# One group of products instead of two for the four finest levels of a gated recurrence, and their four masked copies behind it

## The chip, the cores and the metric

The kernel runs on one core of one Trainium2 chip. What is measured is the time of one execution on the device, in microseconds (us); the time before is the median of three runs. The engines are called PE (TensorE), DVE (VectorE), ACT (ScalarE), POOL (GpSimd) and SP (SyncE).

## The reference

The model is a chain of layers over 256 positions of width 2048: a convolution mixer, a gated recurrence (HGRN2), a sliding-window attention and a gated feed-forward. The change is in the recurrence. It has 16 heads of 128 channels and runs over the positions forward and backward:

```
b = cumsum(log_f)                                  # per channel
decay[t, s] = exp(b[t] - b[s]) where s <= t        # per channel
scores[t, s] = sum_k q[t, k] * key[s, k] * decay[t, s, k]
out[t] = sum_s scores[t, s] * v[s]                 # and the state of the chunks before
```

What is computed is one 256 x 256 matrix of weights per head (lower triangle from the forward pass, upper one from the backward pass, the sum of both on the diagonal), times v. Around it stand a projection in front (q, two gates, v and an output gate z from the normed input), a norm per head, the product with silu(z), and a projection behind.

## The kernel before, in words

Every weight matrix comes in chunks of 256 rows by 512 columns (SP's DMA into `raw`). ACT rounds a chunk to `w_hi` (L928), DVE subtracts to get the rest `w_lo` (L1319), and PE multiplies: three products for each of four pieces, `w_hi` with the high part of the activations (L662), `w_lo` with it (L663), and `w_hi` with their low part (L664). That is 12 products of 512 columns a chunk. There are four slots. PE waits for `split_ready`, ACT for `chunk_used` of four chunks before.

Each phase of the kernel is a `stream` of chunks, 32 in one pass of the recurrence's projection, and each engine runs the same stream. Other work hangs on it by hand: `Hooks().put(tick, step)` makes an engine do a step right behind its own work on chunk number `tick`. The order on each engine is therefore fixed, and engines meet by semaphores only. ACT and DVE can be up to some three chunks ahead of PE.

The recurrence works on four heads at a time, a head group j. While the projection of head group j + 1 (for the last one: of z) streams through PE, `process(j)` is hooked in. The weight matrix of a head is built by halving: level 1 is the block between the two halves of 128 positions, level 2 that between quarters (64), and so on down to neighbours (level 8, `LEVELS` = 64 to 1 for s = 2 to 8); level 0 is the diagonal. The steps of a level s >= 2 are:

- DVE `diffs` (L1567 to L1570) writes differences of the summed gates for queries and keys into one of four operand buffers, `operands(s)` in `E` and `E_more`; ACT `exp` (L1138) exponentiates them; DVE `weigh` (L1578) multiplies the queries by q.
- PE `level(j, s)` (L777) makes 32 small products (four heads, two halves, four quarters of 32 rows; for s = 2 16 of 64) into bank `2 + s % 2` of the PSUM tile `T`, columns 0 to 255. It waits for `weigh` (`g_G`), for the keys' exponentials (`g_K`), and for the copies out of the bank up to level s - 2 (`g_S`).
- A copy takes the level out of PSUM: for levels 0 to 3 on ACT (L1144 to L1155), for levels 4 to 8 DVE `take` (L1586, L1587). The latter is a drain, a memset of two elements and a copy under a mask into the blocks `SB`; a level's mask picks its elements.

When all five are in, ACT `blocks` (L1163, four copies) puts `SB` into the weight matrices `ST`. PE multiplies these by v: `av_across` (L787), which needs only level 1, and `av` (L789), which needs the blocks.

PE's ticks are: level 0 at 8, level 1 at 13, level 2 at 14, levels 3 and 4 at 18, 5 and 6 at 22, 7 and 8 at 26, then `av_across` at 26 and `av` at 28. DVE's `weigh` of level s is at 11 + 2s, its `diffs` of level s + 1 at 12 + 2s, its copies are at 21 (level 4), 25 (5 and 6, before the `weigh` of 7) and 29 (7 and 8). ACT's `exp` of level s is at 11 + 2s, `blocks` at 29. DVE's quarters of the next head group (L1628) are at 28, 30 and 31. For the last head group DVE's first gate of the output (L1644) is at 29, behind the copies.

Of the kernel before, what the change touches and what calls it, by code (L numbers as in the profile page):

```python
# [36 lines left out]
S = 256  # L37
# [22 lines left out]
QUARTER = P // 4  # L60
# [4 lines left out]
ACT_TAKES = 4  # L65
# [111 lines left out]
def build(nc, t, out):  # L177
    ph = phases()
    ctx = ExitStack()
    with ctx:  # L180
# [3 lines left out]
        def sem(name):  # L184
            return ctx.enter_context(nc.semaphore(name))
# [102 lines left out]
        T = ctx.enter_context(nc.psum_tensor("T", [P, 4, 512], F32))  # L288
# [3 lines left out]
        def operands(s):  # L292

            b = (s - 1) % 4 if s else 1
            return (E_more if b >= 2 else E)[:, b % 2, :, :, :]

        def gate_banks(k):
            return T01 if k % 2 else T23
# [19 lines left out]
        g_raw, g_q, g_M, g_act, g_lb, g_D, g_E, g_G, g_mm, g_S = (  # L318
            sem(f"hgrn_{s}") for s in ("raw", "quarters", "moved", "act", "lb", "D", "E", "G", "mm", "S"))
# [287 lines left out]
        def _(pe):  # L607
# [86 lines left out]
            def v_turn(j):  # L694
                if is_first(j):
                    pe.wait_ge(small_in, 16)
                pe.wait_ge(c_v, j + 1)
                if not is_first(j):
                    pe.wait_ge(c_pad, 2 * j)
                transposes(T01, atok, c_T)  # L700
# [43 lines left out]
            at = Hooks().put(4, lambda: v_turn(3))  # L744
# [11 lines left out]
            def level(j, s):  # L756

                pe.wait_ge(g_G, 9 * j + s + 1)
                if s == 0:
                    pe.wait_ge(g_M, 3 * j + 3)  # L760
                if s >= 2:
                    pe.wait_ge(g_K, 7 * j + s - 1)
                    pe.wait_ge(g_S, 9 * j + s - 1)
                e = operands(s)
                for h in range(HPG):
                    for b in range(2):
                        if s == 1:
                            last = nc.tensor.matmul(T[:, h // 2, (h % 2) * S + b * P:(h % 2) * S + b * P + P],  # L768
                                                    e[:, 0, h, b * P:(b + 1) * P], e[:, 1, h, (1 - b) * P:(2 - b) * P],
                                                    start=True, stop=True)  # L770
                            continue
                        n = HB if s == 2 else QUARTER
                        for i in range(P // n):
                            at = b * P + i * n
                            to = b * P + (i ^ 1) * n if s in (2, 3) else at
                            g, q = (e[:, 1, h, at:at + n], qT[:, h, to:to + n]) if s == 0 else (e[:, 0, h, at:at + n], e[:, 1, h, to:to + n])
                            last = nc.tensor.matmul(T[i * n:(i + 1) * n, 2 + s % 2, (2 * h + b) * n:(2 * h + b + 1) * n],  # L777
                                                    g, q, start=True, stop=True)
                last.then_inc(g_mm, 1)

# [11 lines left out]
            def av_across(j):  # L792
                pe.wait_ge(g_raw, 4 * j + 4)
                pe.wait_ge(g_S, 9 * j + 2)
                av_products(True)

            def av(j):
                pe.wait_ge(g_sb, j + 1)
                av_products(False).then_inc(g_av, 1)

            def process(j):

                at = Hooks().put(8, lambda: level(j, 0))
                for s in range(1, 9):
                    at.put(13 if s == 1 else 10 + 4 * (s // 2 + s % 2) if s > 2 else 14, lambda s=s: level(j, s))
                return at.put(26, lambda: av_across(j)).put(28, lambda: av(j))

            def qaai(j):
# [14 lines left out]
            at = process(3)  # L823
# [61 lines left out]
            at = Hooks().put(14, k_turn)  # L885
# [412 lines left out]
        def _(dve):  # L1298
# [4 lines left out]
            def settle():  # L1303

                return nc.vector.drain()  # L1305
# [114 lines left out]
            at = Hooks()  # L1420
# [59 lines left out]
            at = Hooks()  # L1480
# [14 lines left out]
            def bounds_of(j):  # L1495

                if not is_first(j):
                    dve.wait_ge(g_act, 6 * j)
                V.tensor_copy(lbj[:, :, :, :], lbt[:, :, :, bass.ds(4 * j, 4)]).then_inc(g_lb, 1)

            def diagonal_f(j):

                dve.wait_ge(g_lb, j + 1)
                dve.wait_ge(g_act, 6 * j + 1)
                for h in range(HPG):
                    V.tensor_scalar(E[:, 1, 1, h, :], kf[:, h, :], lbj[:, 0, 1, h:h + 1], None, ALU.mult)
                settle()

            def diagonal_b(j):

                dve.wait_ge(g_act, 6 * j + 3)
                for h in range(HPG):
                    last = STT(out=E[:, 1, 1, h, :], in0=kb[:, h, :], scalar=lbj[:, 1, 1, h:h + 1],
                               in1=E[:, 1, 1, h, :], op0=ALU.mult, op1=ALU.add)
                last.then_inc(g_G, 1)

            def scan_f(j):

                dve.wait_ge(g_act, 6 * j + 2)
                for h in range(HPG):  # L1520
                    V.tensor_tensor_scan(Bc[:, h, :], Bc[:, h, :], Bc[:, h, :], 0.0, ALU.add, ALU.bypass)

            def scan_b(j):

                dve.wait_ge(g_act, 6 * j + 4)
                lf = lf_back
                for h in range(HPG):
                    V.tensor_tensor_scan(Xc[:, h, 1:S], lf[:, h, 0:S - 1], lf[:, h, 0:S - 1], 0.0, ALU.add, ALU.bypass)
                V.memset(Xc[:, :, 0:1], 0.0)
                settle()  # L1530

            def keys(j, d):

                dve.wait_ge(g_act, 6 * j + 5 + d)
                if d == 0:
                    TT(kf[:, :, :], kf[:, :, :], Bc[:, :, :], ALU.subtract)
                else:
                    TT(kb[:, :, :], kb[:, :, :], Xc[:, :, :], ALU.add)
                    V.tensor_scalar(back[:, 0, :], Bc[:, :, P - 1], -1.0, None, ALU.mult)
                    V.tensor_scalar(back[:, 1, :], Xc[:, :, P], -1.0, None, ALU.mult)  # L1540
                    settle().then_inc(g_D, 1)
# [30 lines left out]
            def weigh(j, s):  # L1572

                e = operands(s)
                dve.wait_ge(g_E, 8 * j + s)
                if s == 1:
                    dve.wait_ge(g_M, 3 * j + 3)
                TT(e[:, 1, :, :], e[:, 1, :, :], qT[:, :, :], ALU.mult).then_inc(g_G, 1)  # L1578

            def take(j, s):  # L1580

                settle()
                if s == ACT_TAKES:
                    dve.wait_ge(g_S, 9 * j + s)
                dve.wait_ge(g_mm, 9 * j + s + 1)
                V.memset(none[:, :], 0.0)  # L1586
                V.copy_predicated(SB[:, :, :, :].rearrange("p a b c -> p (a b) c"),  # L1587
                                  lmask[:, s - ACT_TAKES, :].unsqueeze(1).to_broadcast([P, 8, QUARTER]),
                                  T[:, 2 + s % 2, 0:S].rearrange("p (a c) -> p a c", c=QUARTER)).then_inc(g_S, 1)

            def o_norm(j):
                dve.wait_ge(g_o, 2 * (j + 1))
# [12 lines left out]
            def process(j, scale_later=0):  # L1605
                at = Hooks().put(1, lambda: bounds_of(j)).put(3, lambda: diagonal_f(j)).put(5, lambda: scan_f(j)).put(6, lambda: diagonal_b(j)).put(9, lambda: scan_b(j))
                at.put(10, lambda: keys(j, 0)).put(11, lambda: keys(j, 1)).put(12, lambda: diffs(j, 2))
                for s in range(1, 9):
                    if s > ACT_TAKES and s % 2:
                        for done in range(max(ACT_TAKES, s - 2), s):  # L1610
                            at.put(11 + 2 * s, lambda done=done: take(j, done))
                    at.put(11 + 2 * s, lambda s=s: weigh(j, s))
                    if 2 <= s < 8:
                        at.put(12 + 2 * s, lambda s=s: diffs(j, s + 1))
                at.put(29, lambda: take(j, 7)).put(29, lambda: take(j, 8))
                return at.put(32, lambda: o_norm(j)).put(33 + scale_later, lambda: o_scale(j))

            def rest(j):
                return Hooks() if isinstance(j, int) and j < 0 else process(j).later(32)
# [31 lines left out]
            at = Hooks().put(32, lambda: z_lo(0)).with_(process(3, 1)).with_(rest(2))  # L1651
# [135 lines left out]
            at = Hooks()  # L1787
# [49 lines left out]
            at = Hooks().put(2, lambda: u_out(FJ - 1)).put(3, lambda: f_quarters(FJ - 1)).put(13, lambda: f_lo_out(FJ - 1))  # L1837
# [52 lines left out]
```

## Time and profile before

| | us |
|---|---|
| median of three runs | 1887.22 (1886.92 to 1888.4) |
| the profiled execution | 1887.1 |
| its span, first to last instruction | 1885.3 |
| PE busy | 1880.2 |
| DVE busy | 1313.4 |
| ACT busy | 1065.9 |
| POOL busy | 689.0 |

The clock granted to PE was full over the whole span. The four head groups stand in the trace at about 477 to 544, 576 to 644, 675 to 743 and 775 to 843 us. A product of fp32 operands, as L777, L787 and L789 make them, stands in the trace as two records, each with its own load of weights, so a level of 32 products is 64 records. Times in the rows are the starts from the span's beginning; ends of products are modelled, and a product of 512 columns is shown as 0.39 us long though the next one starts sooner. "issue" means that nothing shown was waited for.

### The profile page before, as it was taken

Reading aid. Unit: us, or ns where it says so; the run is one execution under the profiler, and the core shown is the slowest. Engines: PE = TensorE matmul, PEld = TensorE weight load, DVE = VectorE, ACT = ScalarE, POOL = GpSimd, SP = SyncE. Lnnn points to the kernel's source line nnn. Section 1 sums busy time; section 2 is a strip of 40 time slices with the busy share of each in tenths; the row PEclk is TensorE's granted clock in tenths of the full one; section 3 lists DMA queues with packets and bytes.
Section 4 is the critical chain, followed back from the end, with each engine's and each line's share of the span. In section 5 each row is a group of like instructions: output and inputs, shape, how many; then the busy total and the mean of one; then the engine's idle time right before and its main releaser. Section 6 shows DMA issues by size and latency. Waiting matters only on the chain.

```text
span 1885.3 us, 29572 instructions
## 1 busy us (share of the span) xinstructions
PE 1880.2 (100%) x11192; PEld 1552.3 (82%) x11192; DVE 1313.4 (70%) x1887; ACT 1065.9 (57%) x1408; POOL 689.0 (37%) x749
## 2 busy tenths in 40 slices
PE   9999999999999999999999999999999999999999
PEld 8888878888888888888887888888888888888887
DVE  5899988746888888887668887655555555544443
ACT  7444466546878787975455756444444444443332
POOL 1899884606051423302418647322222222210000
PEclk9999999999999999999999999999999999999999
DMA  9666656666555565555565455666666666665664
GB/s 328 193 190 190 179 175 201 194 191 179 173 172 170 159 180 167 178 160 177 190 196 151 153 185 176 207 198 189 190 196 193 191 196 192 192 195 192 194 195 159
DMA packets 183603, 352.69 MB, mean 187 GB/s; under 512 B 11840, under 2 KB 12352, under 8 KB 183488
## 3 DMA queue, kind: packets, MB, share of 16 engines
q1 hardware_dynamic: 183344, 351.12, 61.1%
q8 instruction: 75, 1.23, 0.3%
q14 instruction: 40, 0.33, 0.1%
q10 hardware_dynamic: 144, 0.01, 0.0%
HBM read 348.99 MB, written 2.10 MB: 186 GB/s over the span
## 4 chain that ended last, share of the span: by engine, by line
PE 99%; DVE 1%; issue 0%; ACT 0%; POOL 0%; DVEq 0%; POOLq 0%
PE acc L662 32%; PE acc L664 31%; PE acc L663 31%; PE T L777 1%; PE T L613 1%; PE acc L629 1%; PE T L859 0%; PE T L882 0%; PE T L787 0%; PE T L789 0%; PE T L768 0%; PE T L620 0%; DVE cy L1444 0%; DVE w_lo L1319 0%; PE T L736 0%; PE T L725 0%
## 5 line engine op out<-in xcount | busy, mean ns | idle before, releaser
L1319 DVE TENSOR_TENSOR w_lo<-raw,w_hi 128x1024 fp32r<-128x1024 f32 x564 | 702.3, 1248 | 495.7 <-ACT w_hi L928 485.8
L928 ACT ACTIVATE w_hi<-raw 128x1024 fp32r<-128x1024 f32 x655 | 686.9, 1057 | 589.2 <-PE acc L664 565.1
L662 PE MATMUL acc<-w_hi,h_hi 128*128 128x512 f32 x1872 | 734.2, 392 | 0.0
L664 PE MATMUL acc<-w_hi,h_lo 128*128 128x512 f32 x1872 | 728.7, 389 | 0.0
L663 PE MATMUL acc<-w_lo,h_hi 128*128 128x512 f32 x1872 | 728.6, 389 | 0.0
L662 PEld LDWEIGHTS acc<-w_hi,h_hi 128*128 128x128 f32 x1872 | 351.4, 188 | 76.4 <-issue 3.3
L664 PEld LDWEIGHTS acc<-w_hi,h_lo 128*128 128x128 f32 x1872 | 351.3, 188 | 73.6
L663 PEld LDWEIGHTS acc<-w_lo,h_hi 128*128 128x128 f32 x1872 | 351.5, 188 | 71.4
L602 POOL COPY fT<-fq 32x256 f32<-32x256 f32 x176 | 111.7, 635 | 360.0 <-DVE fq L1822 353.1
L502 POOL TENSOR_TENSOR w_lo<-raw,w_hi 128x1024 fp32r<-128x1024 f32 x76 | 181.0, 2412 | 62.5 <-ACT w_hi L928 62.3
L1410 DVE SCALAR_TENSOR_TENSOR T<-vpad,feat,T 128x256 f32<-128x256 f32 x464 | 182.4, 480 | 0.0
L662 PE MATMUL acc<-w_hi,y_hi 128*128 128x512 f32 x384 | 150.5, 392 | 0.4 <-DVE y_lo L1324 0.4
L663 PE MATMUL acc<-w_lo,y_hi 128*128 128x512 f32 x384 | 149.5, 389 | 0.0
L662 PE MATMUL acc<-w_hi,f_hi 128*128 128x512 f32 x352 | 136.9, 389 | 0.0
L663 PE MATMUL acc<-w_lo,f_hi 128*128 128x512 f32 x352 | 136.9, 389 | 0.0
L664 PE MATMUL acc<-w_hi,f_lo 128*128 128x512 f32 x352 | 136.9, 389 | 0.0
L540 POOL COPY kf<-sz 32x256 f32<-32x256 f32 x64 | 37.3, 583 | 249.2 <-DVEq L1305 246.7
L664 PE MATMUL acc<-w_hi,hy_lo 128*128 128x512 f32 x256 | 99.7, 389 | 0.0
L662 PEld LDWEIGHTS acc<-w_hi,y_hi 128*128 128x128 f32 x384 | 72.1, 188 | 16.8 <-DVE y_lo L1324 1.1
L663 PEld LDWEIGHTS acc<-w_lo,y_hi 128*128 128x128 f32 x384 | 72.1, 188 | 14.7
L663 PEld LDWEIGHTS acc<-w_lo,f_hi 128*128 128x128 f32 x352 | 66.1, 188 | 13.8
L664 PEld LDWEIGHTS acc<-w_hi,f_lo 128*128 128x128 f32 x352 | 66.1, 188 | 13.7
(268 smaller groups left out, 1642.7 us busy)
## 6 DMA issues: line engine op xcount, KB each, us to landing
raw<-in_hgrn_w_in_dram SPq DMA_DIRECT2D x160, 512.0 KB, 3.7
raw<-in_conv_w_in_dram SPq DMA_DIRECT2D x96, 512.0 KB, 4.3
raw<-in_ffn_w_gate_dram SPq DMA_DIRECT2D x88, 512.0 KB, 4.4
raw<-in_ffn_w_up_dram SPq DMA_DIRECT2D x88, 512.0 KB, 4.2
raw<-in_ffn_w_down_dram SPq DMA_DIRECT2D x88, 512.0 KB, 4.4
raw<-in_attn_w_qkv_dram SPq DMA_DIRECT2D x40, 512.0 KB, 3.8
raw<-in_conv_w_out_dram SPq DMA_DIRECT2D x32, 512.0 KB, 4.4
raw<-in_hgrn_w_out_dram SPq DMA_DIRECT2D x32, 512.0 KB, 4.4
```

The source lines that it names most:

```text
L502: nc.gpsimd.tensor_tensor(w_lo[:, slot, :, :], raw[:, slot, :, :], rounded(w_hi[:, slot, :, :]), ALU.subtract).then_inc(split_ready, 1)
L540: last = nc.gpsimd.tensor_copy(turned_block(dst, a, b), own_block(src, a, b))
L602: last = nc.gpsimd.tensor_copy(turned_block(fT, a, b), own_block(fq, a, b))
L613: last = nc.tensor.transpose(dst[:, q // 2, at:at + P], src[:, tb, q * P:(q + 1) * P], ident[:, :])
L629: last = nc.tensor.matmul(acc[:, 0, tb, :], stationary[:, n * CK + kk, a], moving[:, n, kk, :], start=first and kk == 0, stop=False)
L662: nc.tensor.matmul(o, hi[:, kt, a], w_hi[:, slot, kk, :], start=c == 0 and kk == 0, stop=False)
L663: nc.tensor.matmul(o, hi[:, kt, a], w_lo[:, slot, kk, :], start=False, stop=False)
L664: last = nc.tensor.matmul(o, lo[:, kt, a], w_hi[:, slot, kk, :], start=False, stop=c == p.chunks - 1 and kk == CK - 1)
L777: last = nc.tensor.matmul(T[i * n:(i + 1) * n, 2 + s % 2, (2 * h + b) * n:(2 * h + b + 1) * n], g, q, start=True, stop=True)
L928: A(w_hi[:, slot, :, :], raw[:, slot, :, :], ACT.Copy).then_inc(hi_ready, 1)
L1319: TT(w_lo[:, slot, :, :], raw[:, slot, :, :], rounded(w_hi[:, slot, :, :]), ALU.subtract).then_inc(split_ready, 1)
L1410: STT(out=cy[:, kt, :] if tap == TAPS - 1 else y, in0=v, scalar=w, in1=y, op0=ALU.mult, op1=ALU.add).then_inc(c_tap, 1)
```

## The change

Levels 5 to 8 all stand at PE's tick 26; 3 and 4 stay at 18. Levels 7 and 8 write to columns 256 to 511 of their banks (`level_at`), where 5 and 6 write to 0 to 255. From level 6 on PE waits only for the copies up to level 4. DVE's copies of levels 5 to 8 all stand at tick 29, each waiting for the products of level 8; the copy of level 4 stays at tick 21.

```diff
+        def level_at(s):
+            return S if s in (7, 8) else 0
...
-                    pe.wait_ge(g_S, 9 * j + s - 1)
+                    pe.wait_ge(g_S, 9 * j + min(s, 6) - 1)
...
-                            last = nc.tensor.matmul(T[i * n:(i + 1) * n, 2 + s % 2, (2 * h + b) * n:(2 * h + b + 1) * n],
+                            last = nc.tensor.matmul(T[i * n:(i + 1) * n, 2 + s % 2, level_at(s) + (2 * h + b) * n:level_at(s) + (2 * h + b + 1) * n],
...
-                    at.put(13 if s == 1 else 10 + 4 * (s // 2 + s % 2) if s > 2 else 14, lambda s=s: level(j, s))
+                    at.put(13 if s == 1 else (18 if s < 5 else 26) if s > 2 else 14, lambda s=s: level(j, s))
...
-                dve.wait_ge(g_mm, 9 * j + s + 1)
+                dve.wait_ge(g_mm, 9 * j + (9 if s >= 5 else s + 1))
...
-                                  T[:, 2 + s % 2, 0:S].rearrange("p (a c) -> p a c", c=QUARTER)).then_inc(g_S, 1)
+                                  T[:, 2 + s % 2, level_at(s):level_at(s) + S].rearrange("p (a c) -> p a c", c=QUARTER)).then_inc(g_S, 1)
...
-                    if s > ACT_TAKES and s % 2:
+                    if s == 5:
                         for done in range(max(ACT_TAKES, s - 2), s):
                             at.put(11 + 2 * s, lambda done=done: take(j, done))
...
-                at.put(29, lambda: take(j, 7)).put(29, lambda: take(j, 8))
+                for s in range(5, 9):
+                    at.put(29, lambda s=s: take(j, s))
```

## Rows read from the trace of the kernel before

**Rows 1.** Page, part 1: busy time, share of the span and instructions.

```profile
PE 1880.2 (100%) x11192; PEld 1552.3 (82%) x11192; DVE 1313.4 (70%) x1887; ACT 1065.9 (57%) x1408; POOL 689.0 (37%) x749
```

**Rows 2.** Page, part 4: the chain that ended last, share of the span by line.

```profile
PE acc L662 32%; PE acc L664 31%; PE acc L663 31%; PE T L777 1%; PE T L613 1%; PE acc L629 1%; PE T L859 0%; PE T L882 0%; PE T L787 0%; PE T L789 0%; PE T L768 0%; PE T L620 0%; DVE cy L1444 0%; DVE w_lo L1319 0%; PE T L736 0%; PE T L725 0%
```

**Rows 3.** Waits of PE, whole span: us in total, times, longest.

```profile
PE T L620 <- POOL ones L490: 1.1, 1, 1.1
PE acc L662 <- DVE y_lo L1324: 0.4, 1, 0.4
```

**Rows 4.** Timeline of PE, level 0 alone: start, us, engine, line, tiles.

```profile
576.38 0.39 PE L664 MATMUL acc<-w_hi,h_lo 128*128 128x512 f32 x1
576.70 0.76 PE L777 MATMUL T<-qT,E 128*32 128x32 f32 x64
...
577.74 0.39 PE L663 MATMUL acc<-w_lo,h_hi 128*128 128x512 f32 x1
```

**Rows 5.** Timeline of PE, levels 5 and 6, second head group.

```profile
620.03 0.39 PE L664 MATMUL acc<-w_hi,h_lo 128*128 128x512 f32 x1
620.35 1.36 PE L777 MATMUL T<-E 128*32 128x32 f32 x128
621.64 0.50 PE L662 MATMUL acc<-w_hi,h_hi 128*128 128x512 f32 x1
621.98 0.40 PE L663 MATMUL acc<-w_lo,h_hi 128*128 128x512 f32 x1
...
624.54 0.39 PE L662 MATMUL acc<-w_hi,h_hi 128*128 128x512 f32 x1
```

**Rows 6.** Waits of PE's weight loads, 470 to 880 us.

```profile
PEld T L777 <- issue: 5.6, 16, 0.4
PEld T L777 <- DVE E L1578: 1.4, 4, 0.4
```

**Rows 7.** Timeline of DVE, second head group, from chunk 25's w_lo to the last copies.

```profile
623.71 1.22 DVE L1319 TENSOR_TENSOR w_lo<-raw,w_hi 128x1024 fp32r<-128x1024 f32 x1
...
627.25 1.22 DVE L1319 TENSOR_TENSOR w_lo<-raw,w_hi 128x1024 fp32r<-128x1024 f32 x1
...
631.93 1.22 DVE L1578 TENSOR_TENSOR E_more<-E_more,qT 128x1024 f32<-128x1024 f32 x1
...
635.69 1.37 DVE L1319 TENSOR_TENSOR w_lo<-raw,w_hi 128x1024 fp32r<-128x1024 f32 x1 [0.19 <-issue]
...
637.26 0.45 DVE L1587 COPY_PREDICATED SB<-lmask,T 128x256 f32<-128x256 int32 x1
637.90 0.44 DVE L1587 COPY_PREDICATED SB<-lmask,T 128x256 f32<-128x256 int32 x1 [0.20 <-issue]
```

**Rows 8.** Timeline of ACT, second head group.

```profile
629.71 2.27 ACT L1138 ACTIVATE E_more<-E_more 128x1024 f32<-128x1024 f32 x2 [1.07 <-DVE E_more L1568]
631.88 1.99 ACT L928 ACTIVATE w_hi<-raw 128x1024 fp32r<-128x1024 f32 x2
638.38 1.70 ACT L1163 ACTIVATE ST<-SB 32x256 f32<-32x256 f32 x4 [4.51 <-DVE SB L1587]
```

**Rows 9.** Timeline of PE, second head group: levels 7 and 8, across, av.

```profile
632.79 1.36 PE L777 MATMUL T<-E_more 128*32 128x32 f32 x128
...
641.46 1.95 PE L789 MATMUL T<-vtok,ST 128*128 128x128 f32 x16
```

**Rows 10.** Timelines of ACT and PE, fourth head group: blocks and av.

```profile
837.10 1.70 ACT L1163 ACTIVATE ST<-SB 32x256 f32<-32x256 f32 x4 [2.44 <-DVE SB L1587]
...
840.14 1.95 PE L789 MATMUL T<-vtok,ST 128*128 128x128 f32 x16
```

**Rows 11.** DMA queues, 470 to 880 us: packets, MB, share of 16 engines.

```profile
q8 instruction: 29, 0.48, 0.5%
```

**Rows 12.** DMA queues, 1240 to 1640 us.

```profile
q1 hardware_dynamic: 40057, 77.21, 66.2%
q14 instruction: 3, 0.02, 0.0%
```

## What is predicted, and how

> **What bounds the kernel now.** I read the page's busy times first: TensorE (PE) is busy for all but 5 us of the span [rows 1]. The chain that ended last says the same of the path: 94% of it are the three weight products of lines 662 to 664, and PE's small groups make up nearly all of the rest [rows 2]. The waits of PE over the whole span are two, 1.1 and 0.4 us, neither of them in the recurrence [rows 3]. So nothing that VectorE (DVE), ScalarE (ACT) or a DMA does in the recurrence is waited for today. A change there can gain only what it takes out of PE's own stream, and can lose only by making PE wait where it now does not.
>
> **What PE pays now for a group of products.** Between weight products PE's starts are 0.227 us apart (0.68 for three), so a chunk of 12 takes 2.72 us. A stretch with a group in it, less these regular steps, is the price of the group. One level: from the L664 at 576.38 to the L663 after the next L662 at 577.74 is 1.36 us, less two steps (0.45) is 0.91 us [rows 4]. Two levels: 620.03 to 621.98 is 1.95, less 0.45 is 1.50 us [rows 5]. The second level therefore costs 0.59 us, and what a group costs however few levels it holds is 0.91 - 0.59 = 0.32 us. A piece of it can be seen: the group's first product starts 0.32 us after the last weight product instead of 0.23, and the first weight product behind it takes 0.34 us to the next instead of 0.23. The loads of weights show it too: PE's loader stood idle 0.35 us before 20 groups, 7.0 us in all [rows 6]. Behind a group of two the first steps are also a little long (0.24 us at first), back to 0.227 after some ten: 621.98 to 624.54 is 11 steps in 2.56 us instead of 2.49, so 0.07 us more [rows 5]. Behind one level there is no such tail in the rows.
>
> **The change, part by part.** (a) Levels 5 and 6 leave tick 22 and join 7 and 8 behind chunk 26 (levels 3 and 4 stay at 18, as 1, 2 and 0 stay). In each of the four head groups one L777 group out of five goes. Its 64 products stay (they stand as 128 records), at 0.59 us a level; only the fixed 0.32 us goes. The tail of 0.07 us goes if the larger group has the same tail; if tails add up, nothing. I take 0.32 plus nearly half of the tail: 0.35 us. Four times: 1.4 us. Below, the fixed cost can't be under the 0.20 us that the two long steps alone show (0.09 + 0.11), 0.8 us in all; above, 0.39 x 4 = 1.6 us.
>
> The Trainium skill weighs this otherwise: "TensorE: Matmul & The Clock Gate", section "Wait — 56ns, not 53.3ns?", has starts of products never closer than about 25 ns. With 32 products to a level that would be an estimated 0.80 us a level, a fixed cost of 0.11 us and a gain of 0.4 us in all. The rows disagree (0.59 us a level, about 18 ns a product), and the measurement decides.
>
> (b) The two masked copies of levels 5 and 6 leave DVE's tick 25 and stand before those of 7 and 8 at tick 29. A drain, a memset and a copy come to 0.65 us from one to the next, so 1.30 us moves [rows 7]. Nothing is added or taken away. DVE has no idle time of note from chunk 25 to 29 in the second head group (0.2 us gaps are the drains), so everything in between moves 1.3 us forward: w_lo of 26 at 627.25, weigh of level 8 at 631.93, w_lo of 29 at 635.69 [rows 7]. ACT allows that: it stood idle 1.07 us for level 8's differences, which come 1.3 us sooner, and its w_hi of 28 and 29 end at 633.87, later 632.7, against a w_lo of 29 at 634.4 [rows 8]. So the four copies start at 635.96 instead of 637.26 and end at 638.36, where the two ended at 638.34.
>
> (c) What the copies wait for. All four now wait for level 8 on PE. PE arrives at chunk 26's end 1.5 us earlier (the group at 22 is gone): the group starts at 632.79 - 1.54 = 631.25 and its four levels end at about 631.25 + 4 x 0.59 + 0.2 = 633.8, 2.1 us before DVE asks. Queued behind the copies on DVE are the w_lo of chunk 30, and on ACT, behind its blocks (which wait for all copies), the w_hi of 30.
>
> (d) What PE itself now meets earlier, having no stop at 22. Chunk 25 starts at 625.7 instead of 627.24; its w_lo ends at 624.93: 0.77 us to spare, the least of this part. Chunk 26 starts at 628.4; w_lo of 26 ends at 627.17 after the move of (b). Level 8 comes at 631.25 + 3 x 0.59 = 633.0; its weigh ends at 633.15 - 1.30 = 631.85. Without the move it would end 0.1 us too late: (b) is what pays for (a). The wait that levels 7 and 8 had on the copies of 5 and 6 is gone because they have the upper halves of the two banks; it was met long before anyway.
>
> (e) The end. ACT's four block copies run from 638.38 to 640.08, and PE asks for them at 641.46 [rows 8, 9]: 1.38 us to spare, after the change 1.0 us. In the fourth head group the blocks end at 838.80 and PE asks at 840.14: 1.34 us [rows 10]. The first gate of the output stands behind the copies there; the turn on PE that needs it comes after L789 and one more chunk of 2.72 us. In the second head group POOL starts its copies as soon as DVE's first transposes are out: 1.3 us sooner, with nobody waiting.
>
> **Sum.** The profiled execution took 1887.1 us (span 1885.3 and 1.8 around it). Less 1.4: 1885.7. The median of the runs shown is 1887.22, 0.1 above it, so 1885.8 us. 0.2% of this kernel is 3.8 us, about what a measurement can tell from no change: the forecast is "the same".
>
> **Rivals.**
> A. The fixed cost belongs to each level and not to the group. Then nothing is gained: 1887.2. Rows 4 and 5 speak against it, since two levels are not twice one.
> B. The copies come late. If DVE does not get forward after tick 25, they end 1.30 us later, the blocks end at 641.38, and PE, there at 641.11, waits 0.27 us in the second head group and by the same sum 0.31 in the fourth [rows 8 to 10]. Four times 0.3 is 1.2 us, and nearly all of the gain goes: 1887.0. It turns into a loss only where the copies are over 1.34 us later than now, which is more than the two moved ones last. For it: the masked copies run while POOL copies, where a w_lo takes 1.37 instead of 1.22 us [rows 7]. Against it: the masked copies themselves, beside POOL, are 0.65 us apart as at tick 25.
> C. Slower: PE's instructions run short. Each product stands as two loads and two products; a group of four levels is 512 instructions in about 2.4 us, and 32 of the across products behind them; today it is 256 and 32 [rows 9]. PE's stream is fetched in pieces of 16 KB (0.48 MB in 29 packets), each 1.1 us of one DMA engine (0.5% x 16 x 410 / 29) [rows 11]. If each of two pieces had to be waited for in full, a group would cost 2.3 us more: 4 x (2.3 - 0.35) = 7.8, so 1895.0. It decides once PE holds less ahead than the run is long. Against it: from 1240 to 1640 us PE goes round its feed-forward loop, at least 384 instructions, with no such packet at all [rows 12], so it holds more than that; and the runs of 256 have no gap. The Trainium skill, "Runtime: NRT & Kernel Launch", section "Instruction fetch mechanics", gives PE room for 2048 instructions in one sentence and only two pieces of 256 in another: by the first nothing happens, by the second this rival would.
> D. Faster by more than 0.2%: it would take waits of PE in the recurrence that the rows do not show. Say 1883.
>
> **Chances.** Forecast 0.76, A 0.07, B 0.09, C 0.05, D 0.03. Only D is faster by over 0.2%, only C slower: faster 0.03, same 0.92, slower 0.05. The range: the gain's ends put the forecast at 1885.4 to 1886.5; A and B end at 1887.2 to 1887.5, and medians of three wander by half a microsecond: 1884.8 to 1887.9.
>
> **What would show it.** PE's rows in each head group: groups of products at ticks 8, 13, 14, 18, 26 and none at 22; the one at 26 with 256 records over 2.5 us, without a gap inside. PE's loader idle before 16 of them and not 20. DVE: four masked copies 0.65 us apart, the first 2.4 us before ACT's blocks start. L789 with no idle before it. Wrong would be: any PE wait on DVE or ACT in the recurrence (B), a group at 26 that lasts over 3 us (C), or a span unchanged within 0.3 us with one group fewer (A).

## The result: slower, by 14 us

| | before | after |
|---|---|---|
| median, four runs each | 1887.16 us (1886.92 to 1888.4) | 1901.17 us (1899.38 to 1903.69) |
| ratio, 95% interval | | 1.0074 [1.0061, 1.0086] |
| the profiled execution, its span | 1887.1, 1885.3 | 1899.38, 1897.6 |

Forecast was 1885.8 us, in 1884.8 to 1887.9, with a chance of 0.05 for slower. The result is slower and outside the range. It is rival C: PE's instructions run short.

In the code of after the lines named here have numbers higher by 3: L662 to L664 are L665 to L667, L777 is L780, L787 is L790, L789 is L792, L1587 is L1590. The page of after, busy times [rows 1]:

```profile
PE 1882.8 (99%) x11192; PEld 1556.8 (82%) x11192; DVE 1312.9 (69%) x1887; ACT 1065.8 (56%) x1408; POOL 685.9 (36%) x749
```

The same instructions and nearly the same busy time in a span 12.3 us longer. The chain by engine; before has 0% at "issue":

```profile
PE 99%; DVE 1%; issue 1%; ACT 0%; POOL 0%; DVEq 0%; POOLq 0%
```

The waits of PE over the whole span of after [rows 3] name the place at once (us in total, times, longest):

```profile
PE T L780 <- issue: 8.1, 3, 2.7
PE T L790 <- issue: 1.7, 1, 1.7
PE T L623 <- POOL ones L493: 1.1, 1, 1.1
PE acc L665 <- DVE y_lo L1327: 0.4, 1, 0.4
```

Two rows are those of before. The two new ones are four gaps, one to a head group, 9.8 us in all, and no engine, no semaphore and no DMA of data ended them. No row names DVE or ACT in the recurrence, so rival B isn't in it. The timeline of PE shows where the gaps are (start, us; idle before in brackets). Second head group of after [rows 9]:

```profile
632.88 0.39 PE L667 MATMUL acc<-w_hi,h_lo 128*128 128x512 f32 x1
633.20 1.36 PE L780 MATMUL T<-E 128*32 128x32 f32 x128
634.41 1.27 PE L780 MATMUL T<-E_more 128*32 128x32 f32 x112
638.40 0.44 PE L780 MATMUL T<-E_more 128*32 128x32 f32 x16 [2.72 <-issue]
638.77 3.29 PE L790 MATMUL T<-vtok,ST 128*128 128x128 f32 x16
641.82 0.47 PE L665 MATMUL acc<-w_hi,h_hi 128*128 128x512 f32 x1
642.13 0.39 PE L666 MATMUL acc<-w_lo,h_hi 128*128 128x512 f32 x1
```

PE stops in the middle of level 8, between two products that wait for nothing (all operands of the level were there when its first product ran). The same rows of the first, third and fourth head group of after:

```profile
534.97 0.94 PE L790 MATMUL T<-vtok,ST 128*128 128x128 f32 x6
537.56 1.27 PE L790 MATMUL T<-vtok,ST 128*128 128x128 f32 x10 [1.65 <-issue]
...
737.70 1.02 PE L780 MATMUL T<-E_more 128*32 128x32 f32 x90
741.37 0.55 PE L780 MATMUL T<-E_more 128*32 128x32 f32 x38 [2.65 <-issue]
741.85 2.05 PE L790 MATMUL T<-vtok,ST 128*128 128x128 f32 x16
...
839.46 0.83 PE L780 MATMUL T<-E_more 128*32 128x32 f32 x67
843.03 1.08 PE L780 MATMUL T<-E_more 128*32 128x32 f32 x61 [2.75 <-issue]
844.04 3.07 PE L790 MATMUL T<-vtok,ST 128*128 128x128 f32 x16
```

Counted from the group's first record the gaps come after 262 (128 + 128 + 6), 240, 218 and 195 records: 22, 22 and 23 earlier from head group to head group. A record is one product and one load, two instructions. A head group's stretch of the stream has 912 records, 1824 instructions, so from gap to gap it is 1824 - 44 = 1780 that the trace shows. 7 x 256 = 1792, if a head group has 12 instructions without a record (waits, say; no row shows them). The queue of rows 11 agrees: from each gap to the next it brings exactly 7 packets of 16 KB. So the gaps seem to sit at one fixed place modulo 256 instructions, at the borders of the pieces in which PE's stream is fetched. Whether the place is a matter of the count alone can be tested.

The second loss is the clock. Windows of after around the second gap (us, busy time and count of PE, PEld, DVE, ACT and POOL, then granted clock, DMA share, GB/s):

```profile
633.00:638.40 5.40, 2.68 (x242) 2.37 (x241) 4.58 (x5) 1.57 (x2) 2.02 (x3) 0.96 0.67 195
638.40:642.00 3.60, 3.60 (x33) 3.53 (x33) 1.77 (x8) 0.90 (x3) 3.22 (x10) 0.58 0.52 154
642.00:650.00 8.00, 8.00 (x45) 6.91 (x44) 5.14 (x6) 3.54 (x5) 5.24 (x11) 1.00 0.34 84
```

Behind a gap of 2.72 us in which PE did nothing the granted clock is 0.58 over 3.6 us, most of them at the lower of its two levels (1.2 of 2.4 GHz), and the across products take 3.29 us where they took 2.05. The fourth head group shows 0.60; the first and the third have a gap too and no such fall.

**Where the 12.3 us went.** The price of the group at 26, by the rule of rows 4 and 5 (from the last weight product in front to the second behind, less two steps), is 3.28 us in each head group of before, and 1.50 for the group at 22 (1.61 in the first). In the second head group of after it is 642.13 - 632.88 - 0.45 = 8.80. The four are 6.30, 8.80, 7.34 and 8.80, 31.2 together, against 19.2 before: +12.0. Of this the gaps are 9.8. The clock is 1.4 in each of two head groups: 8.80 - 7.34 = 1.46 between neighbours with gaps of 2.72 (or 2.75) and 2.65. Another 0.2 us goes with each gap at a full clock too: e3 below has a group of 256 records without a gap for 2.57 us, and three with one for 2.76 to 2.79 beyond the length of the gap. In part it is the first products behind the gap, which are slow (third head group, 38 records in 0.48 us instead of 0.36). The merger itself gives back 4 x 0.30: in the first head group, ahead of the gap, L780 starts at 532.48 and L790 at 534.97, 2.49 us for four levels, where before has 1.29 for two (533.50 to 534.79) and 1.50 for the others. 9.8 + 2.8 + 0.8 - 1.2 = 12.2, against the 12.0 of the groups. The run with the profile is the shortest of the four of after; the median has 1.8 us more, which no trace shows.

### The profile page after: what moved, and what is told of

Same layout as the page of the kernel before. It is cut to its first block, busy times and chain, and to the rows that moved or that the text cites. A ratio compares the mean times of both kernels' runs of the same rounds, so it can differ in the third digit from the quotient of the medians.

```text
span 1897.6 us, 29566 instructions
## 1 busy us (share of the span) xinstructions
PE 1882.8 (99%) x11192; PEld 1556.8 (82%) x11192; DVE 1312.9 (69%) x1887; ACT 1065.8 (56%) x1408; POOL 685.9 (36%) x749
## 4 chain that ended last, share of the span: by engine, by line
PE 99%; DVE 1%; issue 1%; ACT 0%; POOL 0%; DVEq 0%; POOLq 0%
PE acc L665 31%; PE acc L667 31%; PE acc L666 31%; PE T L780 1%; PE T L616 1%; PE acc L632 1%; PE T L790 1%; PE T L862 0%; PE T L885 0%; PE T L792 0%; PE T L771 0%; PE T L623 0%; DVE cy L1447 0%; DVE w_lo L1322 0%; PE T L739 0%
## 5 line engine op out<-in xcount | busy, mean ns | idle before, releaser
L665 PE MATMUL acc<-w_hi,h_hi 128*128 128x512 f32 x1872 | 733.6, 392 | 0.0
L667 PE MATMUL acc<-w_hi,h_lo 128*128 128x512 f32 x1872 | 728.7, 389 | 0.0
L665 PEld LDWEIGHTS acc<-w_hi,h_hi 128*128 128x128 f32 x1872 | 351.5, 188 | 76.0 <-issue 3.3
L667 PEld LDWEIGHTS acc<-w_hi,h_lo 128*128 128x128 f32 x1872 | 351.4, 188 | 73.3
L665 PE MATMUL acc<-w_hi,y_hi 128*128 128x512 f32 x384 | 150.5, 392 | 0.4 <-DVE y_lo L1327 0.4
L665 PE MATMUL acc<-w_hi,f_hi 128*128 128x512 f32 x352 | 136.9, 389 | 0.0
L667 PE MATMUL acc<-w_hi,f_lo 128*128 128x512 f32 x352 | 136.9, 389 | 0.0
L667 PE MATMUL acc<-w_hi,hy_lo 128*128 128x512 f32 x256 | 99.7, 389 | 0.0
L665 PEld LDWEIGHTS acc<-w_hi,y_hi 128*128 128x128 f32 x384 | 72.1, 188 | 16.8 <-DVE y_lo L1327 1.1
L665 PEld LDWEIGHTS acc<-w_hi,f_hi 128*128 128x128 f32 x352 | 66.1, 188 | 13.8
L667 PEld LDWEIGHTS acc<-w_hi,f_lo 128*128 128x128 f32 x352 | 66.1, 188 | 13.8
```

Of the source, the lines that this page charges most:

```text
L665: nc.tensor.matmul(o, hi[:, kt, a], w_hi[:, slot, kk, :], start=c == 0 and kk == 0, stop=False)
L667: last = nc.tensor.matmul(o, lo[:, kt, a], w_hi[:, slot, kk, :], start=False, stop=c == p.chunks - 1 and kk == CK - 1)
```

## The experiments

The theory is rival C in a sharper form: PE has only one piece of instructions in hand, a refill takes about 4 us, and a gap stands at the border of a piece. Against it stand rival B (the moved copies make PE late), and that the group itself is at fault, by the bank halves or by so many small products in a row. e1, e2, e3 and e5 are one run each, beside one run of the kernel before of 1887.71 us; e9 is one run too.

### e1: all of the change but PE's order

```diff
-  (18 if s < 5 else 26) if s > 2 else 14
+  10 + 4 * (s // 2 + s % 2) if s > 2 else 14
```

> The changed kernel with PE's ticks put back (levels 5 and 6 at 22, 7 and 8 at 26); the upper halves of the banks, the shorter wait for the copies and all four copies at tick 29 stay. Theory (PE's instruction stream is fetched in pieces of 256 instructions, only one piece ahead, and a refill takes about 4 us, so a run of over 256 instructions in under 4 us runs dry): no gap in any group, 1887.2 +- 0.7 us. Rival (the copies at 29 or the shared halves make PE wait, or take its clock down): still 1896 us or more.

Measured: 1887.5 us against 1887.71, span 1885.7. PE's waits, whole span:

```profile
PE T L623 <- POOL ones L493: 1.1, 1, 1.1
PE acc L665 <- DVE y_lo L1327: 0.4, 1, 0.4
```

The copies at tick 29, their wait for level 8 and the upper halves of the banks cost nothing. B is out, and the bank halves with it. The loss comes only with PE's order.

### e2: after, with 32 small products more ahead of everything

```diff
+                for i in range(32):
+                    nc.tensor.matmul(T[0:QUARTER, 1, 0:QUARTER], ones[:, 0:QUARTER], ones[:, 0:QUARTER], start=True, stop=True)
```

They run once, in the warm-up at the start, and nothing reads them: 128 instructions that shift the rest of the stream by half a piece.

> The changed kernel with 32 more small products (64 records, 128 instructions of PE with their weight loads) in the warm-up at the start; nothing else. In the changed kernel PE stood still in the group at 26 after 262, 240, 218 and 195 product records in the four head groups. Theory: the gap sits at a fixed place of the instruction stream modulo 256, so it moves 64 records forward: after 198, 176 and 154 records in the first three; in the fourth the place at 131 is reached with its piece in hand (the one before was crossed 6 us before the group) and the gap is after 259, in the across products. Rival 1 (data of level 7 or 8, or a copy, is late): gaps at the old places. Rival 2 (PE stops after a length of run): the same distance from the start of the group as before. Time by the theory 1900 to 1903 us.

Measured: 1904.64 us, span 1902.8. The gaps came after 199, 177, 154 and 259 records. First, second and fourth head group of e2, timeline of PE:

```profile
534.83 0.86 PE L782 MATMUL T<-E_more 128*32 128x32 f32 x71
539.01 0.70 PE L782 MATMUL T<-E_more 128*32 128x32 f32 x57 [3.32 <-issue]
...
638.99 0.62 PE L782 MATMUL T<-E_more 128*32 128x32 f32 x49
642.68 1.29 PE L782 MATMUL T<-E_more 128*32 128x32 f32 x79 [3.07 <-issue]
...
846.12 0.60 PE L792 MATMUL T<-vtok,ST 128*128 128x128 f32 x3
849.05 1.38 PE L792 MATMUL T<-vtok,ST 128*128 128x128 f32 x10 [2.32 <-issue]
```

128 + 71 is 199, and so on. Products that ran 500 us before move the gaps in the recurrence by the 64 records that they are (63, 63 and 64), and the one that falls off one end comes in at the other. Were the group itself at fault, they would have stayed at their product. This run decides for a fixed place in the stream. The time came out 1.6 us above the forecast of 1900 to 1903: three of the gaps are longer than in after (3.32, 3.07 and 3.20 us), and the clock fell behind three of the four (all but 3.20), 0.61 over 539 to 543 us.

### e3: before, with levels 5 and 6 multiplied twice

```diff
-                for h in range(HPG):
+                for h in (*range(HPG), *(range(HPG) if s in (5, 6) else ())):
```

The second pass writes the same values again. Nothing else of the change is there.

> The kernel before, with the products of levels 5 and 6 at tick 22 made twice (same results, 64 more products a head group); copies, banks and all else as before. 128 more records at 9.2 ns are 1.2 us a head group, 4.7 us in all. Theory: the group at 22 is now 512 instructions and runs dry in the head groups where a piece ends 30 to 250 instructions behind its start: counted from the gaps of the changed kernel, gaps of about 2.6 us in the first (after some 180 records), the second (some 160) and the fourth (some 240), and 0 to 0.5 in the third. 1887.2 + 4.7 + 8 = 1900 us, more if the granted clock falls. Rivals (late data, copies, shared halves of a bank): 1891.9 us, no gap.

Measured: 1900.98 us, span 1899.2. First head group of e3, timeline of PE at tick 22:

```profile
521.72 1.83 PE L777 MATMUL T<-E 128*32 128x32 f32 x184
526.39 0.82 PE L777 MATMUL T<-E 128*32 128x32 f32 x72 [2.84 <-issue]
```

Gaps of 2.84, 2.76 and 2.64 us in the first, second and fourth head group, 8.2 in all, none in the third, where the text allowed 0 to 0.5. The doubled levels cost 4 x 1.18 = 4.7, and 1887.7 + 4.7 + 8.2 = 1900.6. So a run of 512 instructions gets its gap with the code of before, in another place of the stream and without bank halves. The queue confirms the size of a piece: 4 x 256 more instructions, and its page has 79 packets of the instruction queue where before has 75. The granted clock stayed at 1.0 all through.

### e5: three levels behind 26 instead of four

```diff
-  (18 if s < 5 else 26) if s > 2 else 14
+  (18 if s < 5 else 22 if s == 5 else 26) if s > 2 else 14
```

> The changed kernel with level 5 alone at tick 22 and levels 6, 7 and 8 at 26: as many groups as the kernel before, the largest of 384 instructions and the 32 of the across products. Theory: the first crossing of a piece's end in the group must be 4 us ahead of the second one. Gaps of about 1.9 us in the first head group (after 198 records, in the across products), 2.5 us in the second (after 176), 1.4 us in the third (after 154) and none in the fourth, where the pieces end 6 and 262 instructions behind the start: 1887.2 + 5.8 = 1893.0 us. Rival (late data or copies): all four head groups alike.

Measured: 1898.99 us, span 1897.2. Waits of PE:

```profile
PE T L780 <- issue: 5.7, 2, 3.5
PE T L790 <- issue: 2.3, 1, 2.3
```

The places were right, after 198, 176 and 154 records and none in the fourth head group. The lengths were not: 2.30, 2.26 and 3.47, 8.0 in all. And in the first two head groups the clock fell (0.53 over 538.2 to 541.8 and over 640.6 to 644.2; the across products of the second took 3.67 us), while behind the longest gap it did not. A refill is not a fixed length (below); why the third one was the longest stays open. The total was missed by 6 us.

### e4 and e8: levels 5 and 6 one or two chunks ahead of 7 and 8

```diff
-  (18 if s < 5 else 26) if s > 2 else 14
+  (18 if s < 5 else 25 if s < 7 else 26) if s > 2 else 14
```

In e8 the 25 is a 24. One chunk between the groups lasts 2.72 us, two 5.44.

> The changed kernel with levels 5 and 6 at tick 25 and 7 and 8 at 26: the same 512 instructions, with one chunk of weight products (24 instructions, 2.72 us) between the two halves; copies at 29 and halves of the banks as in the changed kernel. Theory (pieces of 256 instructions, one ahead, some 4 us to refill): two crossings are now 4.1 us or more apart, so no gap over 0.3 us: 1887.3 us, -0.3 to +0.8 against the kernel before (the fixed cost of the second group is back). Rival (late data or copies because PE reaches chunk 26 earlier): most of the 14 us stays.

> The changed kernel with levels 5 and 6 at tick 24 and 7 and 8 at 26: two chunks (5.4 us) between the two halves. With one chunk between them one gap of 1.8 us was left, in the first head group, where the packet of instructions started late. Theory: the pieces' ends are now over 7 us apart, no gap: 1887.3 us, within 0.7 us of the kernel before. Rival (something else of the changed kernel costs time): over 1888.5 us.

Measured, e4: 1889.36 us (1888.48 to 1889.95) against 1887.28, ratio 1.0009 [1.0, 1.0019]. e8: 1887.42 (1887.03 to 1887.82) against 1887.39, ratio 0.9999 [0.999, 1.0009]. e4 kept one gap, in the first head group, which its text had ruled out; e8 has none. First head group of e4:

```profile
535.24 0.94 PE L790 MATMUL T<-vtok,ST 128*128 128x128 f32 x6
538.00 1.27 PE L790 MATMUL T<-vtok,ST 128*128 128x128 f32 x10 [1.83 <-issue]
```

The gap is after the same 6 records of L790 as in after: same count, same border. With one chunk between, three of four head groups are rid of their gap, with two chunks all. The 512 instructions are the same; what counts is how densely they follow one another.

**The refill, step by step.** With the borders known, the packets of the instruction queue can be laid beside them. Border 2 is the one 128 records ahead of the gap; its time is read off the timeline (second head group of after: 112 records into the 128 of the row at 633.20, 1.06 us later):

```
                     border 2   packet of the        PE goes on   border 2 to
                     on PE      instruction queue    (border 3)   going on
after, head group 1  533.75     535.05 to 536.13     537.56       3.8 us
after, head group 2  634.26     635.88 to 637.07     638.40       4.1
after, head group 3  737.34     739.11 to 740.07     741.37       4.0
after, head group 4  838.88     840.56 to 841.46     843.03       4.2
e4,    head group 1  534.01     535.58 to 536.69     538.00       4.0
```

These rows fit one account. When PE crosses a border, the piece after the next border is asked for: 1.3 to 1.8 us until its packet starts, 0.9 to 1.2 for the packet, 1.3 to 1.6 until PE goes on, 4.0 us together. The other runs spread more, from border 2 to going on: e2 4.7, 4.6, 4.6 and 4.2 us, e3 4.2, 4.1 and 4.0, e5 4.5, 3.7 and 4.9; there the packet starts 1.3 to 2.3 us behind the border and takes 0.9 to 1.7. The piece in hand, 128 records of 32 columns, lasts 1.2 us, and 4.0 less 1.2 is about the gap of 2.7. The first head group's lasts 2.2 us, since six of its records are of 128 columns, which leaves 1.65. In stretches of weight products (0.227 us a record, 29 us a piece) nothing is late; there a packet can come 4.7 us before PE itself reaches the border (657.12 for one that PE crosses at 661.86), so the side that fetches runs ahead of PE, there by some 20 products. That would explain e4's one gap: the packet for border 2 came only at 530.92 to 531.86, so the fetching side could go on at about 533.3 (1.4 us on, an estimate) and had under 1 us of lead over PE, which crossed at 534.01; only then could the piece behind border 3 be asked for. It would also be why before has no gap with its 256 + 32 instructions: in its first head group it reaches the two borders at 533.56 and 535.56, but the packet had already come at 531.92. The other runs agree: where long products run ahead and a border stands 3 to 12 records into a run of small ones, the next border has no gap, though it is only 1.1 to 1.2 us on (3 in the fourth head groups of e2 and e5, 6 in the first of after, 12 in the third of e3); the fetching side would have passed the first border while the long products ran. Where the first border stood 26 or more records in, the second had its gap each time. That the fetching side waits in this way is inferred from these times; no record shows that side itself.

The Trainium skill, "Runtime: NRT & Kernel Launch", section "Instruction fetch mechanics", has both readings: room for 2048 instructions on PE, and "only 2 cache lines" of 256. What these runs bear out is the second: one piece running and one in hand. Its sentence that crossing a border is "mostly hidden" agrees with before and not with after, where it costs 1.65 to 2.75 us.

### e9: after, with half of the recurrence's weight transfers

```diff
+                kt = 1 if name in ("hgrn", "hgrn_z") else CK
-                    sp.dma_start(raw[:, slot, :, :], W[row:row + CK * P, bass.ds(col, GC)]
+                    sp.dma_start(raw[:, slot, 0:kt, :], W[row:row + kt * P, bass.ds(col, GC)]
```

Half of the weight rows of these two streams are left out of the transfers. Asked: is the refill long because it stands behind weight transfers?

> The changed kernel in which SP loads only the first of the two row tiles of every weight chunk in the recurrence's two projections (256 instead of 512 KB; the other tile is left as it stood, so the result is not the reference's). PE's stream and all waits as in the changed kernel. Theory: the 16 KB of instructions queue behind the weights on the DMA engines, so with half of that traffic the packets start sooner and the gaps shrink, from 1.65 to 2.75 us to some 1.0 to 2.0; places of the gaps unchanged (262, 240, 218, 195 records). If the refill is a fixed latency that owes nothing to the traffic: gaps as before, 9.8 us in all.

Measured: 1897.86 us, span 1896.1. The windows 470 to 900 us of after, and then of e9 (columns as above; DMA share 0.56 and 0.33):

```profile
470.00:900.00 430.00, 420.23 (x3758) 350.90 (x3757) 354.59 (x446) 330.71 (x449) 112.90 (x161) 0.99 0.56 166
```

```profile
470.00:900.00 430.00, 422.08 (x3764) 352.43 (x3763) 355.94 (x448) 330.35 (x449) 114.53 (x163) 0.99 0.33 96
```

Gaps of 1.64, 1.90, 2.44 and 1.94 us, 7.9 in all instead of 9.8, at the same records as in after. Read as in the table, border 2 to going on is 3.8, 3.3, 3.8 and 3.35 us, and the time until the packet starts is 0.9 to 1.1 us, against 1.3 to 2.3 in all the gaps of the runs with full transfers. So half of the transfers are worth some 0.5 us of a refill (4.05 on average in after, 3.6 here), a bit over a tenth, and less than the text forecast; what no transfers at all would leave is not shown. This is one run, and the first gap is as long as in after. Halving the traffic, in any case, doesn't hide a refill. The clock fell here behind the third and fourth gap (2.44 and 1.94 us), and not behind the second (1.90).

### e6 and e7: what a merger gains where the instructions suffice

e6 moves level 1 from tick 13 to 14, to level 2: 48 records, so 96 instructions, in 3 us.

```diff
-                    at.put(13 if s == 1 else 10 + 4 * (s // 2 + s % 2) if s > 2 else 14, lambda s=s: level(j, s))
+                    at.put(10 + 4 * (s // 2 + s % 2) if s > 2 else 14, lambda s=s: level(j, s))
...
-                        at.put((15, 17, 20)[s - 1], lambda s=s: take(j, s))
+                        at.put((16, 17, 20)[s - 1], lambda s=s: take(j, s))
```

e7 puts level 0 there too, from tick 8. For that level 0 gets the operand buffer of level 4 and bank 3, and its copy ACT's tick 15.

```diff
-            b = (s - 1) % 4 if s else 1
+            b = (s - 1) % 4 if s else 3
...
-                at = Hooks().put(8, lambda: level(j, 0))
+                at = Hooks().put(14, lambda: level(j, 0))
```

> The kernel before with level 1 moved from tick 13 to 14, in one group with level 2 (96 instructions), and ACT's copy of level 1 from tick 15 to 16. Tests the fixed cost of a group by itself, with a run too short to empty PE's stream: 0.32 us a head group, 4 x 0.32 = 1.3 us faster, 0.9993 of the kernel before. Rival (the cost sits in the change of products' shape, which stays inside the group): within 0.3 us of the kernel before. Against both: if ACT's copy comes late, PE waits at chunk 17 or 18.

> The kernel before with levels 0, 1 and 2 in one group at tick 14 (224 instructions, less than a piece): level 0 moves from tick 8, level 1 from 13; the diagonal's products stand in level 4's operand buffer and level 0 goes to bank 3, ACT's copies of levels 0 and 1 to ticks 15 and 16. Two groups fewer a head group: 8 x 0.32 = 2.6 us faster, 1885.0 us, ratio 0.9986, without a gap. Rival (shape changes cost, not groups): one level-0 group's 0.32 at most, 1.3 us or less. If the copies come late, PE waits before chunk 16 or 17 and shows it as a wait for DVE's w_lo.

Measured, e6: 1887.97 us (1887.03 to 1889.45) against 1887.28, ratio 1.0003 [0.9994, 1.0012]: no gain that can be told. e7: 1889.27 (1889.01 to 1889.9), ratio 1.0011 [1.0002, 1.002]: slower. Second head group of e6, timeline of PE:

```profile
594.68 0.39 PE L664 MATMUL acc<-w_hi,h_lo 128*128 128x512 f32 x1
594.91 1.95 PE L768 MATMUL T<-E 128*128 128x128 f32 x16
596.79 1.15 PE L777 MATMUL T<-E 128*64 128x64 f32 x32
597.87 0.50 PE L662 MATMUL acc<-w_hi,h_hi 128*128 128x512 f32 x1
598.20 0.40 PE L663 MATMUL acc<-w_lo,h_hi 128*128 128x512 f32 x1
```

By the rule of rows 4 and 5 the merged group costs 598.20 - 594.68 - 0.45 = 3.07 us. In before the two cost 1.79 and 1.28 us, which is 3.07 again. The row at 594.91 hints at why: the products of L768 have the full 128 columns of the array, as the weight products have, and start 0.23 us behind the last of these, a regular step; L777 with its narrow tiles starts 0.32 behind it in every group. What two groups in one save would thus be a change of tile shape in and out, about 0.3 us, and only where both groups have the same narrow shape. e7 fits: 3.96 us against 0.90 + 1.79 + 1.28 = 3.97. The Trainium skill, "TensorEngine Tiling (Array Packing)", section "Key Properties", says that a change of tiling mode drains the engine; the rows agree, and put a size to it.

e7 was forecast at 1885.0 us and lost 2 us, in rival B's way as far as it shows. PE, without a stop at ticks 8 and 13, gets to some chunks sooner than DVE has split them. Waits of PE's weight loads, e7, whole span:

```profile
PEld acc L662 <- DVE w_lo L1320: 2.9, 6, 0.7
```

In before this row reads 0.2 us, one time. The loads run ahead of the products, so not all of it reaches them: four weight products start 0.18 to 0.48 us late, 1.2 us together. The rest of the 2 us is not traced.

## Why the prediction was wrong, step by step

- **What bounds the kernel** (PE alone, nobody waited for): right. It is the reason why every us that PE stands still shows in the time in full.
- **(a) 0.32 us fixed for a group, 0.35 with the tail**: right in size for this merger, 0.30 measured, 1.2 us in all instead of 1.4. What it is was wrong: e6 and e7 merge groups of other tile shapes and save nothing, so it is not the price of a group; it fits that of changing to narrow tiles and back. Rival A is out. (The gain's ends, 1.6 and 0.8, put the forecast at 1885.6 to 1886.4, not at 1885.4 to 1886.5; nothing hangs on it.)
- **(b) to (e), DVE, ACT, the copies and the end**: right as far as the runs show it. In e1, where the copies are moved alone, the first one starts at 636.22, with the trace 0.24 late at that place, so 635.98; forecast was 635.96. In after PE never waits for them either, but the 2.1 us of (c) are gone: the gap holds level 8 back, and the first copy of the second head group starts only at 638.91, just behind the end of that level. The limit that (d) looked for, PE ahead of `w_lo`, is met in e7.
- **Rival C: here the argument failed.** The sum has no term for PE's own instructions: it puts them at nothing, and they cost 9.8 us of gaps and 2.8 of clock. C named them and was dismissed. Its count was right (512 instructions in 2.4 us and 32 behind), its mechanism, and with the borders its condition: "once PE holds less ahead than the run is long". Two sentences threw it away. The first: PE goes round a loop of at least 384 instructions without a packet [rows 12], "so it holds more than that". These rows show what PE keeps of what it has already run, and say nothing of what it has fetched ahead. After and e4 speak to that: their gaps fit one piece of 256. The second: "the runs of 256 have no gap". Two borders can't both lie in 256 instructions, so these runs could not show it (the one in before that holds two, with the 32 of the across products, had its packet early); the run of 512 always has two. The chance of 0.05 rested on these two, and it belonged near one half, as the two readings of the Trainium skill stood against each other and no row decided.
- **C's price**: 2.3 us for a refill, from two packets of 1.1 us. Measured are 1.65 to 2.75, and the packet is only about a quarter of a refill (table). 1895.0 was still 6 us short of the median: 2.8 for the clock, 0.8 for what goes around the gaps and 0.6 for longer gaps make 4.2 of it, the smaller gain 0.2, and 1.8 is what the median has over the profiled run.
- The marks named for C were the right ones: a group at 26 over 3 us, and a gap inside.

No version gained: e1, e6 and e8 can't be told from the kernel before, all others lose. By this account the 1.2 us of the merger can't be had, as a run of 512 instructions always has two borders in it.

**Open.** Why the clock falls behind some gaps and not behind others. It did after 2.72 and 2.75 us (after), 3.32, 3.07 and 2.32 (e2), 2.30 and 2.26 (e5), 2.44 and 1.94 (e9): nine of 19. It did not after 1.65 and 2.65 (after), 3.20 (e2), 2.84, 2.76 and 2.64 (e3), 1.83 (e4), 3.47 (e5), 1.64 and 1.90 (e9). The longest gap of all is among these, so the length of the gap does not decide alone. Open too is why a refill takes 3.7 us in one place and 4.9 in another at the same DMA share.

## What to carry to other kernels

Count the instructions of a run of small products, loads included (an fp32 product is four), and set them against time: here the engine stalled, whatever its operands did, wherever a run reached two borders of 256-instruction pieces less than about 4 us apart, unless the first stood within the run's first dozen records behind many long products (the one chunk of e4 was not enough). Two that were 4.16 us apart (e4, second head group) had no gap. Spread such runs with long products between them, some 5 us to every 256 instructions here, rather than gathering them; gathering saved 0.3 us a group at most. In a profile the mark is an idle time that "issue" ended, inside a group of equal instructions, at a place that shifts with every instruction put in far ahead of it; and a packet of the instruction queue that ends 1.1 to 1.6 us before the engine goes on. A loop that runs without refills says nothing of how far ahead an engine fetches.

## What the runs showed of the hardware

- The gaps fit a PE that has one piece of 256 instructions in hand beside the one it runs (after, e2 to e5). A refill takes 3.7 to 4.9 us with the DMA engines 55 or 56% busy (3.8 to 4.2 in after) and 3.3 to 3.8 with 33% (e9, one run), of which the packet itself is 0.9 to 1.7.
- Behind nine of 19 gaps of 1.6 to 3.5 us the granted clock fell to its lower level for some 3 us (0.58 over 3.6 us in after), which there added half as much again to the loss: 1.4 us to 2.7.
- One group of 32-column tiles less between full ones saved 0.30 us (after); joining a group of 128-column products to narrow ones saved nothing (3.07 us in e6, 1.79 + 1.28 in before).
- The first records behind a gap are slow at a full clock too: in the third head group of after 38 records take 0.48 us (741.37 to 741.85) instead of 0.36.
